# Linear attention in two stages: a branch's products and norm moved, and a chain put ahead of a selection

## What is computed

```python
o = hgrn2_recurrence(q, 1.0 - f, silu(inp), log(f))          # 4 heads of 128, 256 tokens
out_a = rmsnorm(o, hgrn_out_norm) * silu(og)
u = gelu(u)
v = rmsnorm(gelu(v).reshape(B, S, 4, 128), gmlp_v_norm)
w_causal = gmlp_w_s * tril(ones(128, 128))
sv = einsum('gts,bnsgd->bntgd', w_causal, v.reshape(B, 2, 128, 4, 128)) + gmlp_b_s.T[:, :, None]
out_b = u * sv
y = concatenate([out_a, out_b]) @ w_out
```

## Time and profile before

| what | us |
|---|---|
| median of 3 runs | 3181.8 |
| lowest and highest | 3168.32, 3184.36 |
| profiled execution, its own time | 3158.51 |
| its span | 3156.8 |
| TensorE busy | 3089.9 (98%) |
| VectorE busy | 2159.0 (68%) |
| ScalarE busy | 1577.8 (50%) |
| GpSimd busy | 284.1 (9%) |

### The profile page before, as it was taken

The page is one execution under the profiler, slowest core; times in us unless marked ns, Lnnn a source line. Parts: engine busy times, 40 slices in busy tenths (PEclk is TensorE's granted clock), DMA queues, the critical chain, the costliest instruction groups (busy, mean ns, idle before and its releaser), DMA issues. The chain is left out here.

```text
span 3156.8 us, 66323 instructions
## 1 busy us (share of the span) xinstructions
PE 3089.9 (98%) x25784; PEld 3022.7 (96%) x25784; DVE 2159.0 (68%) x3611; ACT 1577.8 (50%) x2733; POOL 284.1 (9%) x194
## 2 busy tenths in 40 slices
PE   9899999999999899999999999999999899999998
PEld 9699999999999799999999999999997799999898
DVE  4559888889997559898878887333255455555654
ACT  5264566655554655576655555222245344454443
POOL 0116300000001006400000000000020010000100
PEclk9899999999998999999999999999999799999999
DMA  5156644478896256644479896333342146555464
GB/s 185 61 158 195 197 146 142 150 256 290 287 353 232 82 158 192 195 152 140 145 258 316 310 318 202 95 98 96 97 116 73 41 152 192 175 189 184 135 193 145
DMA packets 172779, 560.64 MB, mean 178 GB/s; under 512 B 22480, under 2 KB 31440, under 8 KB 172000
## 3 DMA queue, kind: packets, MB, share of 16 engines
q1 hardware_dynamic: 172640, 558.82, 54.4%
HBM read 557.71 MB, written 1.05 MB: 177 GB/s over the span
## 5 line engine op out<-in xcount | busy, mean ns | idle before, releaser
L236 ACT ACTIVATE peer_e_hi<-raw 128x1024 fp32r<-128x1024 f32 x560 | 590.5, 1055 | 376.9 <-PE peer_e_out L1503 307.9
L240 DVE TENSOR_TENSOR peer_e_lo<-raw,peer_e_hi 128x1024 fp32r<-128x1024 f32 x498 | 611.0, 1227 | 176.5 <-ACT peer_e_hi L236 172.1
L240 DVE TENSOR_TENSOR ffn_lo<-raw,ffn_hi 128x1024 fp32r<-128x1024 f32 x256 | 312.9, 1225 | 458.2 <-ACT ffn_hi L236 458.2
L236 ACT ACTIVATE ffn_hi<-raw 128x1024 fp32r<-128x1024 f32 x264 | 279.5, 1062 | 520.4 <-PE ffn_acc L2766 328.6
L1499 PE MATMUL peer_e_out<-x_normed,peer_e_hi 128*128 128x256 f32 x2048 | 493.7, 283 | 0.0
L1500 PE MATMUL peer_e_out<-x_normed,peer_e_hi 128*128 128x256 f32 x2048 | 482.3, 278 | 0.0
L1565 PE MATMUL peer_e_out<-peer_h_pair,peer_e_hi 128*128 128x256 f32 x2048 | 477.8, 276 | 0.4 <-DVE peer_e_lo L240 0.4
L1566 PE MATMUL peer_e_out<-peer_h_pair,peer_e_hi 128*128 128x256 f32 x2048 | 477.7, 276 | 0.0
L1500 PEld LDWEIGHTS peer_e_out<-x_normed,peer_e_hi 128*128 128x128 f32 x2048 | 385.9, 188 | 0.0
L1499 PEld LDWEIGHTS peer_e_out<-x_normed,peer_e_hi 128*128 128x128 f32 x2048 | 385.7, 188 | 0.0
L1565 PEld LDWEIGHTS peer_e_out<-peer_h_pair,peer_e_hi 128*128 128x128 f32 x2048 | 384.5, 188 | 0.7 <-issue 0.7
(11 more groups left out here) (635 smaller groups left out, 6018.8 us busy)
## 6 DMA issues: line engine op xcount, KB each, us to landing
raw<-in_l_down SPq DMA_DIRECT2D x256, 512.0 KB, 3.6
raw<-in_l_up SPq DMA_DIRECT2D x256, 512.0 KB, 4.8
raw<-in_ffn_wi SPq DMA_DIRECT2D x176, 512.0 KB, 3.8
peer_e_ring<-in_w_mod SPq DMA_DIRECT2D x144, 512.0 KB, 5.2
raw<-in_ffn_wo SPq DMA_DIRECT2D x88, 512.0 KB, 3.7
raw<-in_l_peer_w_query SPq DMA_DIRECT2D x32, 512.0 KB, 3.6
raw<-in_w_in SPq DMA_DIRECT2D x26, 512.0 KB, 3.8
l_in_raw<-in_l_w_in SPq DMA_DIRECT2D x24, 512.0 KB, 4.4
```

The lines of the kernel that those rows point to most:

```text
L236: return act.activation(hi, v, ACT.Copy)
L240: return eng.tensor_tensor(lo, v, hi.bitcast(F32), ALU.subtract)
```

## The change

In the recurrence stage: the gated branch's norm factors are made at the start. ScalarE sums the squares of each of the eight 128x128 pieces with its accumulator and takes the root; VectorE inverts it in step 3 (vector_invert); ScalarE scales v by it (scalar_scale). TensorE's eight products go into o_ps, two each in place of the keep-awake products of steps 5, 6 and 7, and two behind the transposes that feed the picks. The norm's gain is applied behind the product, by ScalarE while it copies the result out (scalar_take), since the norm's feature is now along the partitions; for that the gain is stored as four columns too. The bias product is left out; VectorE adds the bias and multiplies with u behind its last pick (vector_gate). TensorE waits for `taken` before it writes o_ps.

In gla: VectorE runs the half s = 1 of the chain before the selection, and waits for `summed` ahead of it. TensorE waits for `copied` in score, and issues score(1) ahead of carried(0).

```diff
--- before.py
+++ after.py
@@ -45,7 +45,7 @@
 
 
 COLS = [
-    ("l0_norm_mix", 8), ("l0_hgrn_out_norm", 4), ("l0_norm_ffn", 8), ("l1_norm_mix", 8),
+    ("l0_norm_mix", 8), ("l0_hgrn_out_norm", 4), ("l0_gmlp_v_norm", 4), ("l0_norm_ffn", 8), ("l1_norm_mix", 8),
     ("l1_mla_cq_norm", 2), ("l1_mla_ckv_norm", 1), ("l1_norm_ffn", 8), ("c_2", 8), ("c_ctx_2", 8),
     ("b_mod_2", 2 * MT), ("norm_g_2", 48), ("b_a_f_2", 2), ("b_a_b_2", 2), ("gla_g_2", 1),
     ("pool_scale_2", 8), ("final_g_2", 8), ("lb_logits", 12), ("l1_mla_q_nope", 1), ("l1_mla_k_nope", 1),
@@ -865,7 +865,6 @@
         head_norms = HeadNorms(st, K, sq[:].rearrange("p h t -> p (h t)"), l_ps[:, 0, 512:512 + AH * TT],
                                a_ps[:].rearrange("p h t -> p (h t)"))
         gmlp = gmlp(st)
-        gmlp_ps = l_ps[:, 1].rearrange("p (g t) -> p g t", t=T)
         at_ps = a_ps[:, 0, 0:AH * TT * HC].rearrange("p (n t) -> p n t", t=HC)
         last_ps = l_ps[:, 0, 0:AH * P].rearrange("p (h t) -> p h t", t=P)
         block = st.ctx.enter_context(nc.Block())
@@ -941,6 +940,8 @@
                     dve.wait_ge(decay, i)
                 else:
                     dve.tensor_copy(cc[:, :, 0:1], fc[:, :, 0:1]).then_inc(cummed, 1)
+                if i == 3:
+                    gmlp.vector_invert(dve)
                 if i >= 2:
                     dve.wait_ge(product, i - 1)
                 dve.tensor_tensor(chunk(pair[:, i % 2])[:, :, 0:i + 1], dst[:, :, 0:i + 1],
@@ -987,7 +988,7 @@
             move(3)
             for n in range(1, LEVELS):
                 pick(n)
-            gmlp.vector_norm(dve)
+            gmlp.vector_gate(dve)
 
             dve.wait_ge(squared, 1)
             for h in range(AH):
@@ -996,7 +997,6 @@
                                                op0=ALU.mult, op1=ALU.mult)
             ins.then_inc(gated_o, 1)
             head_norms.vector(dve)
-            gmlp.vector_gate(dve, gmlp_ps)
             dve.wait_ge(head_norms.spread, 1)
             dve.wait_ge(gated_o, 1)
             dve.tensor_tensor(mix[:, 0:AH], a_ps[:], gated[:], ALU.mult)
@@ -1013,7 +1013,10 @@
                                    chunk(pair[:, i % 2, hs])[:, :, 0:i + 1],
                                    start=i == 0, stop=i == HC - 1, skip_group_check=True)
                 mm.then_inc(product, 1)
-                keep_awake(pe, K, l_ps[:, 0, 0:P], 2)
+                if i < HC - 3:
+                    keep_awake(pe, K, l_ps[:, 0, 0:P], 2)
+                else:
+                    gmlp.tensor(pe, o_ps, 2 * (i - HC + 3), 2 * (i - HC + 4))
 
             def level(n):
                 pe.wait_ge(moved, n + 1)
@@ -1035,6 +1038,7 @@
                 for t in range(TT):
                     mm = pe.transpose(at_ps[:, h * TT + t, :], score[:, h, t * P:(t + 1) * P], K.ident[0:HC, 0:HC])
             mm.then_inc(turned, 1)
+            gmlp.tensor(pe, o_ps, 6, 8)
             for n in range(1, LEVELS):
                 level(n)
             pe.wait_ge(moved, LEVELS + 1)
@@ -1044,6 +1048,7 @@
                 mm = pe.matmul(last_ps[:, h], k_last[:, h], q_last[:, h], start=True, stop=True)
             mm.then_inc(leveled, 1)
             pe.wait_ge(picked, LEVELS + 1)
+            pe.wait_ge(gmlp.taken, 1)
             for h in range(AH):
                 for t in range(TT):
                     pe.matmul(o_ps[:, h, t * P:(t + 1) * P], v[:, t, h * P:(h + 1) * P], att[:, h * TT + t],
@@ -1055,12 +1060,12 @@
             mm.then_inc(out_sum, 1)
             pe.wait_ge(squared, 1)
             head_norms.tensor_sums(pe)
-            gmlp.tensor(pe, gmlp_ps)
             head_norms.tensor_spread(pe)
 
         @block.scalar
         def _(act):
             gmlp.scalar_squares(act)
+            gmlp.scalar_scale(act)
             act.wait_ge(product, HC)
             act.activation(score[:], a_ps[0:HC], ACT.Copy).then_inc(scored, 1)
             for n in range(LEVELS - 1):
@@ -1074,9 +1079,9 @@
             half = HC << (LEVELS - 1)
             act.activation(q_last[:, :, 0:half], qd[LEVELS - 1][:, :, P:P + half], ACT.Copy)
             act.activation(k_last[:, :, half:], kd[LEVELS - 1][:, :, half:P], ACT.Copy).then_inc(kept, 1)
+            gmlp.scalar_take(act, o_ps)
             act.wait_ge(leveled, LEVELS + 1)
             act.activation(att_last[:], last_ps, ACT.Copy).then_inc(across, 1)
-            gmlp.scalar_root(act)
             act.wait_ge(out_sum, 1)
             act.activation(sq[:], o_ps[:], ACT.Square).then_inc(squared, 1)
             head_norms.scalar(act)
@@ -1089,10 +1094,11 @@
 
     def __init__(self, st, K, dram, u, gv, mix):
         self.K, self.dram, self.u, self.gv, self.mix = K, dram, u, gv, mix
-        self.w_in, self.kept, self.squared, self.summed, self.rooted, self.v_step, self.normed, self.mixed = (
-            st.sem(f"gmlp_{x}") for x in ("w_in", "kept", "squared", "summed", "rooted", "v_step", "normed", "mixed"))
+        self.w_in, self.kept, self.squared, self.rooted, self.inverted, self.scaled, self.biased, self.mixed, self.taken = (
+            st.sem(f"gmlp_{x}") for x in ("w_in", "kept", "squared", "rooted", "inverted", "scaled", "biased", "mixed",
+                                          "taken"))
         self.w, self.wc = (st.sb(f"gmlp_{x}", [P, self.GROUPS, P]) for x in ("w", "wc"))
-        self.sq = st.sb("gmlp_sq", [P, TT * self.GROUPS, P])
+        self.sq = st.sb("gmlp_sq", [P, self.GROUPS, T])
         self.ss, self.root, self.rstd = (st.sb(f"gmlp_{x}", [P, TT * self.GROUPS]) for x in ("ss", "root", "rstd"))
         self.g4 = gv[:].rearrange("p n (g d) -> p (n g) d", g=self.GROUPS)
 
@@ -1106,37 +1112,49 @@
                            pattern=[[0, self.GROUPS], [1, P]], channel_multiplier=-1).then_inc(self.kept, 1)
 
     def scalar_squares(self, act):
-        act.activation(self.sq[:], self.g4, ACT.Square).then_inc(self.squared, 1)
-
-    def scalar_root(self, act):
-        act.wait_ge(self.summed, 1)
+        waste = self.sq[:].rearrange("p g (n d) -> p (g n) d", d=P)
+        for i in range(TT * self.GROUPS):
+            ins = act.activation(waste[:, i], self.g4[:, i], ACT.Square, accum_out=self.ss[:, i:i + 1])
+        ins.then_inc(self.squared, 1)
+        act.wait_ge(self.squared, 1)
         act.activation(self.root[:], self.ss[:], ACT.Sqrt, bias=self.K.eps[:], scale=1.0 / P).then_inc(self.rooted, 1)
 
-    def vector_norm(self, dve):
-        chain = Chain(dve, self.v_step)
-        dve.wait_ge(self.squared, 1)
-        dve.tensor_reduce(self.ss[:], self.sq[:], AX_X, ALU.add).then_inc(self.summed, 1)
+    def vector_invert(self, dve):
         dve.wait_ge(self.rooted, 1)
-        chain(dve.reciprocal(self.rstd[:], self.root[:]))
-        chain(dve.tensor_tensor(self.g4, self.g4,
-                                self.rstd[:].unsqueeze(2).to_broadcast([P, TT * self.GROUPS, P]), ALU.mult))
-        dve.tensor_tensor(self.gv[:], self.gv[:], self.K.row("l0_gmlp_v_norm").unsqueeze(1)
-                          .to_broadcast([P, TT, 512]), ALU.mult).then_inc(self.normed, 1)
-
-    def tensor(self, pe, acc):
-        pe.wait_ge(self.kept, 1)
-        pe.wait_ge(self.normed, 1)
-        bias = self.K.row("l0_gmlp_b_s")
+        dve.reciprocal(self.rstd[:], self.root[:]).then_inc(self.inverted, 1)
+
+    def scalar_scale(self, act):
+        act.wait_ge(self.inverted, 1)
+        for i in range(TT * self.GROUPS):
+            ins = act.activation(self.g4[:, i], self.g4[:, i], ACT.Copy, scale=self.rstd[:, i:i + 1])
+        ins.then_inc(self.scaled, 1)
+
+    def tensor(self, pe, acc, first, end):
+        if first == 0:
+            pe.wait_ge(self.kept, 1)
+            pe.wait_ge(self.scaled, 1)
+        for i in range(first, end):
+            g, n = divmod(i, TT)
+            mm = pe.matmul(acc[:, g, n * P:(n + 1) * P], self.gv[:, n, g * P:(g + 1) * P], self.wc[:, g, :],
+                           start=True, stop=True)
+        if end == TT * self.GROUPS:
+            mm.then_inc(self.mixed, 1)
+
+    def scalar_take(self, act, acc):
+        act.wait_ge(self.mixed, 1)
+        gain = self.K.col("l0_gmlp_v_norm")
         for g in range(self.GROUPS):
-            for n in range(TT):
-                out = acc[:, g, n * P:(n + 1) * P]
-                pe.matmul(out, self.gv[:, n, g * P:(g + 1) * P], self.wc[:, g, :], start=True, stop=False)
-                mm = pe.matmul(out, self.K.ones[0:1, :], bias[0:1, g * P:(g + 1) * P], start=False, stop=True)
-        mm.then_inc(self.mixed, 1)
-
-    def vector_gate(self, dve, acc):
-        dve.wait_ge(self.mixed, 1)
-        dve.tensor_tensor(self.mix[:, 4:8], acc[:], self.u[:], ALU.mult)
+            ins = act.activation(self.sq[:, g], acc[:, g], ACT.Copy, scale=gain[:, g:g + 1])
+        ins.then_inc(self.taken, 1)
+
+    def vector_gate(self, dve):
+        bias = self.K.row("l0_gmlp_b_s").rearrange("p (g t) -> p g t", g=self.GROUPS).unsqueeze(2)\
+            .to_broadcast([P, self.GROUPS, TT, P])
```

(18 more changed lines are left out.)

## The result

The changed kernel takes 3144.7 us (median of 20 executions, 3129.3 to 3176.5). The kernel before, timed beside it, takes 3168.5 us (median of 20, 3153.4 to 3185.7). The medians lie 23.8 us apart. The ratio is 0.9937, with a 95% interval from 0.9914 to 0.9959: 20 us less, between 13 and 27. Set against the forecast of 12.9 us less this is more, and past the 0.5% where I had put only 0.36. The stated range (3156 to 3181) was missed by two things: the reference time itself was 3168.5 and not 3181.8 once more runs were made (13 of the 24 us between 3168.9 and 3144.7), and the change gives more than the sum, 11 us more by the medians and 7 by the ratio.

The account below looks back on a forecast made before the run. TensorE, busy for 98% of the span, was taken as the bound. The recurrence's -9.8 us and gla's -3.1 us summed to -12.9 us, taking the median from 3181.8 to 3168.9 us, range 3156 to 3181.

Parts of the forecast that it names:

- Part 1: Recurrence tail: with the branch's products moved out, the spread starts right behind the reciprocal, 10.06 us less.
- Part 2: Recurrence stage: the eight products' new places, six replacing keep-awake products and two ahead of the second level, cost 0.
- part 4: Recurrence stage: ScalarE's copies out of the bank and VectorE's gate cost 0, with 4.4 us of cover.
- Part 3: Start of recurrence: ScalarE's squares, root and scalings fit its idle; VectorE's reciprocal adds 0.25 us to the path.
- no difference: Recurrence stage: TensorE's clock behaves alike after the change; ends were -1.8 us or +1.5 to +3 us.
- Rival (b): Next stage's start gives back 1.5 to 3 us, reciprocal or step 5's wait up to 1; 3171 to 3173, chance 0.15.
- Part 5: gla: the chain's first half ahead of the selection and the new order remove three TensorE waits, 3.1 us less.
- 0.5 us either way: gla: the swap of score(1) and carried(0) moves work between clocks, making the gain 2.6 to 3.6 us.
- Rival (a): gla: clock stays or comes back high, 2.8 to 6.4 us more gain; 3161 to 3166, chance 0.22.
- Rival (c): gla: at the higher clock the first selection comes 0.9 us late and TensorE with it; 3170 to 3172, chance 0.08.
- The base: Whole kernel: the reference median of 3181.8 us from which the forecast gain was subtracted.

Follow-up runs that it names:

- e2: Only the gla change, on the kernel before; ratio to before 0.9984 (0.9956 to 1.0011), gla 41.5 us.
- e4: The kernel before, unchanged, run once more; recurrence stage 53.9 us, gla 52.5 us.
- e7: Changed recurrence stage with old gla, the branch's eight products put back between sums and spread; stage 49.5 us, ratio 0.9983.
- e8: The kernel before without the eight one-row bias products, bias left out of the result; recurrence stage 44.6 us, ratio 0.9981.
- e15: The kernel before with the tail's eight 128-row products first, then the eight bias products; recurrence stage 53.0 us, ratio 0.9985.
- e1: Only the recurrence stage's change, on the kernel before with old gla; ratio 0.9968 (0.9942 to 0.9994), recurrence stage 43.8 us.
- e12: The kernel before with only the first half of gla's chain ahead of the selection, second run; gla 49.0 us.
- e5: The kernel before with only score(1) ahead of carried(0) in gla, plus its wait for the copy; gla 44.9 us, ratio 1.0002.
- e13: The kernel before with eight added 128x128 products as a block ahead of carried(0) in gla; gla 51.3 us.
- the first: First trace of the changed kernel, both stages changed against the kernel before; recurrence stage 44.2 us, gla 38.3 us.
- e6: The kernel before with only the first half of gla's chain ahead of the selection, first run; gla 42.4 us, ratio 0.9998.
- e10: The changed kernel with unread products filling TensorE's idle in both tails; ratio to before 0.9957 (0.9932 to 0.9982), gla 43.7 us.
- e3: The changed kernel run again, both stages changed against the kernel before; ratio 0.9934 (0.9904 to 0.9964), gla 41.6 us.

## Why the prediction was right or wrong

The sign was right, the likeliest time and the range were not.

- **Part 1, the products out of the tail: right in size, in part by luck, and wrong in what it is.** I read 10.06 us from the gap between reciprocal and spread. Measured, the spread starts 12.0 us earlier in the stage than in before's first trace, and 9 us earlier than in e2 and e4. I put all of it down to the queue. e7, e8 and e15 show that more than half were the one-row products and the alternation with them, at 0.26 us a change at 1.2 GHz. The trace of before showed it: the two instructions at 129.50 took 0.40 us to the next pair (129.90), when L1049's 16 took 2.05 us.
- **Part 2 and part 4, the new places: right.** The second level's wait behind the last two products shrank from 2.56 to 2.12 us, no more. The four copies took 1.55 us, with 6 us to spare, and VectorE's two operations ended at 123.15, ahead of the squares at 123.82.
- **Part 3, ScalarE's early work: right.** The squares came every 0.29 us with their read-outs, 0.11 faster than the 0.40 that I took from the earlier trace rows, so eight took 2.5 us and not 3.2; the table load took 1.28 us and the root stood right behind it, so of the Trainium skill's 2.66 us (ScalarE: Activation LUTs, What ACT_TABLE_LOAD costs) the trace again shows only the load. The scalings took 2.45 us for eight, against 2.5. The reciprocal cost about 0.2 us.
- **The clock in the recurrence stage: the term "no difference" was too cautious by 1 to 2 us.** The stage gave 11.4 us where the sum had 9.8, and its spread ran in 2.67 us instead of 3.78. I had read the fall at 130 as one behind a short wait; the trace has it at 130.5, 1 us into the branch's products and with TensorE busy since 127.7. Every trace with before's stage has a low stretch of 10 to 17 us over its tail. In the changed kernel it lasts 7 us, half of it in the next stage, or 3.4 (e1). Rival (b), a price in the next stage, didn't come: its start was low for 3.3 to 3.7 us both before and after.
- **Part 5, gla: the step that failed.** The waits did go (1.38 and 1.34 us, and the 0.41), as forecast, and in the traces that begin like the prediction's the chain alone gave 2 us. The term that failed is the clock, which I left at 0.5 us either way for the swap: of the 10 us that both edits gave in those traces, 6 to 7 are clock, and in the traces high at the start both gave 12 to 14, of which 8 to 10 are clock once the waits are taken off. I had also missed that it isn't the swap's alone: at that other beginning the chain alone gave 8 to 10 us, and the wait of 0.41 us that it takes away is one of 2.34 there.
- **Rival (a)** was nearest to what happened, with a chance of 0.22; its 16 to 21 us hold the 20 of the ratio. Its reason, products that follow without a gap, is at best half of it. In the four comparable traces with before's order and in e12, the fall at 23.3 us came out of unbroken work on the carried products, so it wasn't waits that let it fall; with the score products or a dense block ahead (e5, e13), it didn't come there. The Trainium skill's rule (TensorE: Matmul & The Clock Gate, Part 1), that the clock falls after idle, would have given the high clock for another reason; e12's rows stand against that reason, as the earlier trace rows did, while the falls at 10.4 and 13.8 us, behind waits of 2.40 and 2.34 us, go its way.
- **Rival (c)** came true in the traces with the high clock in direction 0 and the chain ahead (the first, e6, e10). In the first, the selection started 1.1 us behind its score (2495.36, the score's end being 2494.3), and TensorE waited 2.40 instead of 1.38 us. In e3, at the low clock, it waited 1.46. It is the price of the chain ahead, and in those traces the second direction gained far more.
- **The base.** I took the median of three runs. Twenty gave 3168.5. A sum of differences should have been given a range as wide as that median is uncertain: its three runs lay 16 us apart, and I allowed 6. With the right base alone, the forecast would have been 3155.6, and the measured time 10.9 us below it.

What stays open: what lets the clock fall. In ten traces it fell within carried products (64 rows by 64 columns) that had no wait just ahead, or up to 0.4 us behind them (e2, the first), but in e13's first direction it didn't, and elsewhere it fell behind waits. Their rows, their columns, and why alternation doesn't keep it weren't taken apart. And traces of the same kernel that differ in where the low stretch begins differ by 1 to 7 us; I compared like with like, and of most kinds there is one only.

## What to carry to other kernels

Where a stage's end is TensorE's, look at the start-to-start time of its products, not only at their number: here products of 128 rows and of one row in turn cost well over half more than in blocks, and the few that only add a bias were half of a tail. When an edit changes the order of TensorE's work, read what it does just before each fall of the granted clock; the order can be worth more than the waits it removes. Compare traces whose clock begins alike; without that e6 would have spoken for one theory and e12 for the other. And a higher clock pays only if the engine that feeds TensorE is not next in line (e13): with the swap alone TensorE still waited 1.77 us before the last carried products at the high clock (e5), and the chain ahead of the selection took that wait away (e2, e3).
